# Hybrid decoder step on one core: the order of outer products and states in the mLSTM heads, and the shape of the normalizer

## What is computed

```
C_new = a_end * C + einsum('bhsd,bhse->bhde', kc * decay, vc)   # state, 512 x 512
n_new = a_end * n + einsum('bhs,bhsd->bhd', decay, kc)          # normalizer, 512
num   = einsum(S, vc) + a * einsum('bhtd,bhde->bhte', qc, C)
qn    = sum(S) + a * einsum('bhtd,bhd->bht', qc, n)
h     = num / max(|qn|, exp(-m))
hc    = h * sigmoid(og);  hn = layernorm(hc)
out   = (hn * out_g + skip * xc) * silu(z)
y     = x + out @ w_out
```

## Time and profile before

| | us |
|---|---|
| median of 3 runs | 1213.54 (1213.1 to 1216.08) |
| the profiled execution, its time | 1211.22 |
| its span, first to last instruction | 1209.5 |
| TensorE busy | 1066.2 (88%) |
| VectorE busy | 622.8 (51%) |
| ScalarE busy | 400.0 (33%) |
| GpSimd busy | 302.9 (25%) |
| mean granted TensorE clock | 0.932 of full speed |

### The profile page before, as it was taken

How to read it: one execution, slowest core, us unless ns; L and a number is a source line. 1 busy time by engine, 2 the same in 40 slices (tenths; PEclk the granted TensorE clock), 3 DMA queues, 4 the chain that set the end, 5 groups by cost and what they waited for, 6 DMA issues and landing times. The chain is left out here.

```text
span 1209.5 us, 15983 instructions
## 1 busy us (share of the span) xinstructions
PE 1066.2 (88%) x6038; PEld 765.1 (63%) x6038; DVE 622.8 (51%) x1050; ACT 400.0 (33%) x705; POOL 302.9 (25%) x208
## 2 busy tenths in 40 slices
PE   5899999996887499997868989988998989986998
PEld 3677777773334289896645576845776576833776
DVE  5645555556475589984325344343435353256332
ACT  4333444423001223342534224431544224512310
POOL 5433444411000233341313123230423123110000
PEclk9999999997898689998978999888998989988999
DMA  8232222244776145473296644856556644944221
GB/s 236 70 89 75 74 73 69 79 157 157 261 298 208 31 90 175 142 240 102 61 325 214 218 131 157 285 176 213 182 190 210 220 131 148 313 164 168 70 70 70
DMA packets 146196, 191.73 MB, mean 159 GB/s; under 512 B 23906, under 2 KB 87250, under 8 KB 144558
## 3 DMA queue, kind: packets, MB, share of 16 engines
q1 hardware_dynamic: 130782, 157.05, 39.5%
q0 software_dynamic: 6000, 24.35, 7.1%
q10 hardware_dynamic: 9344, 9.39, 2.3%
HBM read 135.66 MB, written 55.22 MB: 158 GB/s over the span
## 5 line engine op out<-in xcount | busy, mean ns | idle before, releaser
L2084 PE MATMUL col_ps<-h_hi,ring_hi 128*128 128x260 f32 x448 | 133.7, 298 | 0.0
L2084 PE MATMUL col_ps<-low,ring_hi 128*128 128x260 f32 x448 | 130.4, 291 | 0.0
L2084 PE MATMUL col_ps<-h_hi,ring_lo 128*128 128x260 f32 x448 | 130.3, 291 | 0.0
L1940 DVE SCALAR_TENSOR_TENSOR state<-state,s_all,outer 128x1024 f32<-128x1024 f32 x64 | 84.1, 1348 | 61.8 <-ACT outer L1776 46.5
L629 PE MATMUL pj<-w_hi_a,h_hi_a 128*128 128x512 f32 x256 | 107.2, 419 | 5.7 <-POOL w_lo_a L454 5.6
L629 PE MATMUL pj<-w_lo_a,h_hi_a 128*128 128x512 f32 x256 | 101.8, 398 | 0.0
L629 PE MATMUL pj<-w_hi_a,h_lo 128*128 128x512 f32 x256 | 101.6, 397 | 0.0
L454 POOL TENSOR_TENSOR w_lo_a<-w_in,w_hi_a 128x1024 fp32r<-128x1024 f32 x32 | 77.9, 2458 | 90.5 <-PE pj_s L617 45.8
L2084 PEld LDWEIGHTS col_ps<-h_hi,ring_hi 128*128 128x128 f32 x448 | 89.2, 199 | 16.3 <-issue 16.3
L2084 PEld LDWEIGHTS col_ps<-low,ring_hi 128*128 128x128 f32 x448 | 89.0, 199 | 0.0
L2084 PEld LDWEIGHTS col_ps<-h_hi,ring_lo 128*128 128x128 f32 x448 | 88.4, 197 | 0.0
(11 more groups left out here) (322 smaller groups left out, 2114.5 us busy)
## 6 DMA issues: line engine op xcount, KB each, us to landing
state<-in_state_C SPq DMA_DIRECT2D x64, 512.0 KB, 6.6
out_C_sample<-state SPq DMA_DIRECT2D x64, 512.0 KB, 5.5
w_in<-in_a_w_in SPq DMA_DIRECT2D x64, 256.0 KB, 4.3
ring_raw<-in_m_w_in POOLq DMA_DIRECT2D x28, 512.0 KB, 6.9
shared<-in_m_w_in SPq DMA_DIRECT2D x20, 512.0 KB, 5.1
k_pages<-in_cache_k SPq DMA_DIRECT2D x16, 512.0 KB, 7.8
v_bcast<-keep_v_rows SPq DMA_DIRECT2D x32, 256.0 KB, 8.2
keep_xm_keep<-xm SPq DMA_DIRECT2D x4, 1040.0 KB, 6.6
```

Of the source, the lines that this page charges most:

```text
L1940: nc.vector.scalar_tensor_tensor(out=state[:, i % 4], in0=state[:, i % 4], scalar=s_all[:, 0, h, b:b + 1], in1=outer[:, g], op0=ALU.mult, ...
L2084: last = nc.tensor.matmul(col_ps[:, u % 4, 0:HALF], a[n % RING][:, k, :], b[:, k, s * HALF:(s + 1) * HALF], start=(k == 0 and j == 0), sto ...
```

## The change

It does five things.

- In head 0, samples 0 to 6 are spread: one each behind the first four column tiles (0 to 3), sample 4 among the values, 5 and 6 behind the values, where 0, 1 and 2 stood together behind the first tile.
- In heads 1 to 3, ScalarE's outer product for sample 6 moves ahead of `out_gate(h, 3)`, VectorE's update ahead of the first norm. TensorE's place for it stays.
- VectorE updates sample 0 of the next head ahead of the first two z's and the first two `mix_in`, instead of behind them.
- The normalizer is made by four matmuls with one output row and 512 columns, behind the first `prompt_state`, instead of sixteen with 128 rows and one column. It is copied to the first row of `kd` (the decayed keys, no longer needed then) and stored as one row of 2 KB; the next head's `decayed` waits for that store.
- The zeroing matmul moves from the start of the stage to behind head 0's `values_of`, with the other half of `qm`, which is still zero then. VectorE waits for the first constant itself.

```diff
-        n_out = m.sb("n_out", [P, FH])
+        n_out = kd[0:1, 0, :]
...
@@ ScalarE @@
-                if h == 0:
-                    outer_of(h, 0)
                 cast_tile(n0 + 2)
                 for s in range(NT):
                     factors(h, s)
-                if h == 0:
-                    outer_of(h, 1)
-                outer_of(h, 2)
+                b0 = 2 if h else 0
+                outer_of(h, b0)
                 out_gate(h, 0)
-                outer_of(h, 3)
+                outer_of(h, b0 + 1)
                 out_gate(h, 1)
                 cast_tile(n0 + 3)
                 take_rows(h)
-                outer_of(h, 4)
+                outer_of(h, b0 + 2)
                 out_gate(h, 2)
                 cast_tile(n0 + 4)
-                outer_of(h, 5)
+                outer_of(h, b0 + 3)
+                outer_of(h, b0 + 4)
                 out_gate(h, 3)
...
-                outer_of(h, 6)
+                if h == 0:
+                    outer_of(h, 5)
+                    outer_of(h, 6)
...
-                nc.scalar.copy(n_out[:], q_ps[:, FH:2 * FH]).then_inc(n_taken, 1)
+                nc.scalar.copy(n_out, q_ps[0:1, :]).then_inc(n_taken, 1)
                 act.wait_ge(n_taken, h + 1)
-                act.dma_start(io.n_prompt[h].rearrange("(d p) -> p d", p=P), n_out[:]).then_inc(n_stored, 16)
+                act.dma_start(io.n_prompt[h:h + 1, :], n_out).then_inc(n_stored, 16)
...
@@ VectorE @@
+                if t == 0:
+                    need(dve, n_stored, 16 * h)
...
+            dve.wait_ge(consts, 1)
...
-                new_state(h, 4)
-                new_state(h, 5)
+                new_state(h, b0 + 2)
+                new_state(h, b0 + 3)
+                new_state(h, b0 + 4)
+                if h == 0:
+                    new_state(h, 5)
                 norm_h(h, 0)
                 norm_h(h, 1)
-                new_state(h, 6)
+                if h == 0:
+                    new_state(h, 6)
                 scale_h(h, 0)
...
                 if more:
+                    new_state(h + 1, 0)
                     z(h, 0)
                     z(h, 1)
                 mix_in(h, 0)
                 scale_h(h, NT)
                 mix_in(h, 1)
                 if more:
-                    new_state(h + 1, 0)
                     z(h, 2)
...
@@ TensorE @@
                 if d == 0:
                     pe.wait_ge(*tok_count(h, NUM + NT - 1))
-                for s in range(NT):
-                    last = nc.tensor.matmul(q_ps[:, FH + d:FH + d + 1], kd[:, s, d * P:(d + 1) * P], one[:],
-                                            start=(s == 0), stop=(s == NT - 1))
-                if d == FH - 1:
+                    for s in range(NT):
+                        last = nc.tensor.matmul(q_ps[0:1, :], one[:], kd[:, s, :], start=(s == 0), stop=(s == NT - 1))
                     last.then_inc(n_done, 1)
...
-            pe.wait_ge(consts, 1)
-            nc.tensor.matmul(sn_ps[:], qm[:, 0, 0:2, :].rearrange("p f b -> p (f b)"), xc[:, 0, 0:SEQ], start=True, stop=True)
...
                     pe.wait_ge(xc_in, 16 * h)
+                else:
+                    pe.wait_ge(consts, 1)
+                    nc.tensor.matmul(sn_ps[:], qm[:, 1, 0:2, :].rearrange("p f b -> p (f b)"), xc[:, 0, 0:SEQ],
+                                     start=True, stop=True)
...
                 column(h, 0)
-                if h == 0:
-                    sample_q(h, 0)
-                    sample_q(h, 1)
-                sample_q(h, 2)
+                sample_q(h, b0)
                 column(h, 1)
-                sample_q(h, 3)
+                sample_q(h, b0 + 1)
...
                     if t == 1:
-                        sample_q(h, 6)
+                        sample_q(h, b0 + 4)
+                if h == 0:
+                    sample_q(h, 5)
+                    sample_q(h, 6)
```

13 lines of the change are left out of this document (6 added, 7 removed).

## The result

The changed kernel takes 1162.0 us (median of 4 runs, 1158.6 to 1166.7), the kernel before beside it 1213.3. The ratio is 0.9576 with a 95% interval of 0.9538 to 0.9614: 51 us are gone. The forecast was 1170, with a range of 1160 to 1187. The profiled execution took 1162.85 us, its span is 1161.1 us, against 1209.5 before.

A forecast was written before the change was run, and what follows sets the result against it. TensorE, busy 88% of the span, was taken as the bound, with 38.8 us of waits for state updates. Terms summing to -42.5 from 1211.2 us gave 1168.7, put at 1170 for the median of runs, range 1160 to 1187.

The forecast's parts named there:

- head 0, columns: Head 0, first column tile to first turned gate: spreading the states saves 14.5 us, before a new gate wait of 1.7.
- The gate wait: TensorE newly waits for ScalarE's last gate behind the outer product: 1.7 us in heads 0 to 2, 4.2 in the last, +9.3.
- Next head's state 0: At three changes of head, the update ahead of two z's removes 7.4 us each, -22.3 in all.
- Rival 3: At the change of head, z and mixing reach TensorE's banks late, half of 22.3 comes back: 1181 us, chance 0.06.
- State 6: Between second and third value block, the update ahead of the norms removes 5.5 us in each of four heads, -22.0.
- Head 0's norm: In head 0, state 5 stands ahead of the first norm on VectorE, delaying the third value block: +2.0, bounds 0 and 5.5.
- The clock: Half clock at the change of head goes with its wait; that in the values stays and can lengthen: +1.5.
- rival 1: The waits go but the half clock stays at changes of head and in the values: 1184 us, chance 0.12.
- Normalizer: Four 512-column matmuls replace four groups of 1-column ones: +0.1 us a head, +0.4 in all, bounds -0.5 to +2.5.
- Initial matmul: Moved from the stage's start to behind the value blocks; nothing won at the start, +1.2 us.
- Rival 4: Better than forecast: broadcasts land in 6.5 us and head 0 waits for nothing: 1162 us, chance 0.06.
- Rivals 2 and 5: Data late, 1182 us, chance 0.12; and slower than before, the outer product ahead of the gate bounding all heads, chance 0.02.

The follow-up runs named there:

- e1: Kernel before with only VectorE's update of the next head's state 0 moved ahead of the first two z's: 1189.4 us, ratio 0.9798.
- e2: Kernel before with only head 0's states spread as in the changed kernel: 1199.3 us, ratio 0.9885.
- e3: Kernel before with only state 6 earlier in heads 1 to 3 (outer product ahead of last gate, update ahead of norms): 1196.3 us, ratio 0.9885.
- e9: Kernel before with the three orders together, normalizer still as columns and zeroing matmul still at the start: 1158.8 us, ratio 0.9540.
- e12: Changed kernel with ScalarE's outer product of state 6 (4 in head 0) behind the last gate, the cast and the five copies: 1161.1 us, ratio 0.9553.
- e8: Changed kernel with each state load queued ahead of the broadcast of a v row, so broadcasts go later: 1180.3 us, ratio 0.9730.
- e5: Changed kernel with ScalarE's outer product of state 6 (4 in head 0) directly behind the last output gate: 1161.1 us, ratio 0.9557.
- e4: Changed kernel with the normalizer again as 16 one-column matmuls and its old store: 1159.6 us, ratio 0.9566.

## Why the prediction was right, and where it was off

The forecast's mechanism held: the waits for a state at the changes of head and between the values were worth their length and the restart behind them, less what came in their place, and the three orders add up within the noise (e1, e2, e3, e9). The number was 8 us too high, at the very edge of the forecast's own range of 1162 to 1178, and it would have been further off had its errors not gone both ways. What moved against what was forecast, from the two profiled executions, first matmul of the stage to the first of the output projection (545.7 us before, 493.7 after):

| piece | forecast | measured |
|---|---|---|
| start of the stage (initial matmul) | +1.2 | -1.2 |
| head 0, columns (-14.5, gate +1.7) | -12.8 | -16.1 |
| head 0, values (+1.9 +2.0 -5.5) | -1.6 | +3.1 |
| heads 1 to 3, columns (gate +7.6) | +7.6 | -0.3 |
| heads 1 to 3, values | -16.5 | -15.4 |
| three changes of head | -22.3 | -22.5 |
| columns behind the changes | -0.6 | -1.0 |
| prompt state with normalizer, four heads | +0.4 | +1.3 |
| clock | +1.5 | in the others |
| sum | -43.1 | -52.0 |

Outside the stage the span got 3.6 us longer, where the code is the same (2.2 of it before the stage begins); that gives the 48.4 us between the two spans.

Most of the 8.9 us by which the sums differ are three terms. The gate waits were 5.0 us shorter than said, and the columns of heads 0 to 2 came out another 6 us shorter, as slow stretches went that the forecast had kept; against that, head 0's values took 4.7 us more. The same stage by TensorE's busy time, from the first column tile to the output projection (columns as in the earlier trace rows), before and after:

```profile
599.36:1105.29 505.93, 448.73 (x2596) 310.60 (x2595) 216.01 (x412) 177.59 (x311) 116.50 (x88) 0.92 0.61 199
600.44:1055.53 455.09, 429.34 (x2499) 290.98 (x2498) 216.14 (x412) 179.90 (x313) 115.47 (x88) 0.96 0.65 221
```

Of the 50.8 us saved here, 31.4 were idle time and 19.4 busy time, with nearly the same work. For the idle time the forecast had 38.8 less 9.3 and 2.0, that is 27.5; for the busy time 13.7 for seven restarts, less 1.5 for longer slow stretches and about 1 for the initial matmul.

**Next head's state 0**: right to 0.2 us. The pair was to end before TensorE comes, and does by 1.4 us, the margin that was read (833 against 834.35). Rival 3 (handed on at the change of head) would have shown in e1 as less than 22; it did not.

**State 6**: the gain in the values was right within 1.1 us in the sum, and under-priced: at full clock it is 7.4 us a head (e3), and the changed kernel gives 1.7 us back in heads 1 and 3 and 3.3 in head 2, as stretches at half clock fall on its values again. In head 0 it gained nothing that is left: the wait there went, and the one for the norm came.

**The gate wait, the term that was mis-sized**: +9.3 was forecast, 4.3 measured (1.47, 0.39, 1.13, 1.28); with the outer product out of the way (e12) it is nothing, so these 4.3 us are the product's. The forecast took the median landing of all 32 broadcasts, 8.2 us. Those that count landed in 5.6 (head 0, issued 625.21, outer product at 630.85), 6.8 (head 2, 878.30 and 885.12) and 5.7 us (head 3, 998.27 and 1003.98), although the median of all is still 7.9 us (it was 8.2). In head 1 the product waited for VectorE to free the outer buffer, and the broadcast had landed by then, in 6.1 us or less. Most of all the last head, priced at 4.2, took 1.28. The mechanism itself is shown by e8: the bound is there, but it began later than thought.

**Head 0's norm**: "ready about when the norm would start" was right, +2.0 was too low: 3.28, and 2.7 us of half clock behind it (9.01 instead of 6.28), for which the forecast had no term, 6.0 together. It is the largest error to the other side. VectorE shows the cause, an outer product and then a load, ahead of the norm:

```profile
643.02 1.29 DVE L1942 SCALAR_TENSOR_TENSOR state<-state,s_all,outer 128x1024 f32<-128x1024 f32 x1 [2.39 <-ACT outer L1776]
646.21 1.28 DVE L1942 SCALAR_TENSOR_TENSOR state<-state,s_all,outer 128x1024 f32<-128x1024 f32 x1 [1.90 <-DMA state<-in_state_C]
647.41 0.16 DVE L1957 SCALAR_TENSOR_TENSOR rd<-q_ps,em_col 128x4 f32<-128x4 f32 x1
```

**The clock**: here the forecast was too careful. It had the stretches at half clock stay and lengthen (+1.5), and gave 0.12 to rival 1, in which every slow restart stays. In fact they went from 99 to 65 us in all, and from 74 to 30 between the first column tile and the last head's turned blocks; the start and the end of the stage have 10 us more.

The columns of heads 1 and 2 took 35.2 us before, with slow stretches (766.8 to 775.3 in head 1) at which there was no wait but the 0.9 us for `staged` that every kernel has; e1 and e3 show the same list at 33.65, e5 in two heads at 32.1. The term that failed here is 35.2 us for the columns: the forecast took it for the list's own time, and 1.5 to 3 us of it were the cost of slow stretches.

The Trainium skill (TensorE: Matmul & The Clock Gate, Part 1) says that the penalty is run-variable. The runs agree: the four of e3 have mean clocks from 0.931 to 0.943, and in the traces the values' list takes 15.2 us in two heads of e3 and two of e4 and 16.9 in two of the changed kernel, the same instructions. But the stretches at the changes of head are no matter of chance: all three are gone in e1 and in every later kernel with that order. Behind the gate chance has a part: the four longer waits of e8 have 13.7, 13.7, 6.8 and 10.1 us of half clock from just ahead of the gate to the values, where the changed kernel has 10.0, 3.4, 6.8 and 3.4.

**Normalizer**: +0.3 a head instead of +0.1, within its bounds; four matmuls with one output row take 3.59 us, as long as four full ones. **Initial matmul**: the eight kernels with it behind the values took 38.5 to 40.9 us to the first column (the changed one 38.6), the six with it at the start, the kernel before among them, 38.0 to 39.7: no difference can be shown, so the -1.2 us in the table are not shown to be its doing.

**What would show it**: no wait for a state, head 0 at 34 us where 37 was said, gate waits of 1 to 4 us (three of four over 1), normalizer 3.59, the end of the stage at 1055.5 instead of 1062. "Longest in the last head" was wrong, it was head 0.

Rival 4 (better, 1162) gave the time but only half of the mechanism: the broadcasts that matter did land sooner than its 6.5 us, head 0 did not wait for nothing. Rivals 2 and 5 need late data; e8 shows what this costs, and the changed kernel does not have it.

## What to carry to other kernels

Price a wait of the bounding engine with the restart behind it: what counts is the stretch from the last instruction before it to the first at full speed after it, and removing it gave that back at the changes of head in every kernel here that has the new order (7.8 us for 15.3). Between the values it gave back 7.4 us in the best heads and 5.7 or less in others, as other slow stretches came and went. When a step moves up in a list, look up the landing of the very transfer it will wait for, not the median of its kind; and before moving a step again to save the rest, list what stands behind it on its engine, since the wait goes to the next in line (gate, copy, cast, norm) and the time hardly changes. A queue that issues in order is a lever in one direction: broadcasts issued 2.5 to 4 us later cost 18 us here, and issued earlier they won nothing that could be measured.

## What the runs showed that was not expected

A wait of 3.7 us ahead of light work (transposes and 1-column matmuls) was followed by 13.7 us at a clock of 0.55 (e8, head 1), and one of 4.5 us in e5 by 10.2 us. The 5.5 us waits ahead of dense column tiles in the kernel before were followed by 3.2 us of it: the slow stretch began inside the wait and ended with the sample_q behind it (836.3 to 843.1, with the column tile at 842.77). So the same idle time can cost more where the work behind it is light, but it does not always: in head 2 of e8 a wait of 4.37 us ahead of the same light work was followed by less than 5 us. What decides between the two was not found.

The kernel with state 6 alone scattered over 16 us in four runs, the other new ones over 3 to 12. In e3 and in e9 the shorter runs are those with the higher mean clock (e9: 0.958 and 0.955 at 1154.6 and 1157.0 us, 0.945 twice at 1160.6 and 1161.5); why e3 scatters most stays open.
